# Differential attention: one pair block of scores split into a block for each map

## What is computed

```python
def diff_attention(q, k, v, lam):
    scale = HEAD_DIM ** -0.5

    def block(j, qb):
        logits = jnp.einsum("bqhmd,bkhmd->bhmqk", qb, k).astype(jnp.float32) * scale
        p = jax.nn.softmax(logits, axis=-1)
        a = (p[:, :, 0] - lam * p[:, :, 1]).astype(v.dtype)
        return jnp.einsum("bhqk,bkhd->bqhd", a, v)
...
    q, k = axial_rope(q, ang), axial_rope(k, ang)
...
    o = finish(diff_attention(q, jnp.concatenate([kc, k], axis=1),
                              jnp.concatenate([vc, v], axis=1), lam), s)
    oc = finish(diff_attention(qc, kc, vc, lam), n_ctx) if need_ctx else None
```

## Time and profile before

| | us |
|---|---|
| median of 3 runs | 3616.75 |
| lowest, highest | 3615.14, 3618.65 |
| the profiled execution | 3619.0 |
| its span, first to last instruction | 3617.2 |
| TensorE busy in the span | 3279.7 (91%) |
| VectorE, ScalarE, GpSimd busy | 1588.1, 1343.1, 1172.8 |
| mean granted TensorE clock | 0.946 |

### The profile page before, as it was taken

How to read it: one execution, slowest core, us unless ns; L and a number is a source line. 1 busy time by engine, 2 the same in 40 slices (tenths; PEclk the granted TensorE clock), 3 DMA queues, 4 the chain that set the end, 5 groups by cost and what they waited for, 6 DMA issues and landing times. The chain is left out here.

```text
span 3617.2 us, 51819 instructions
## 1 busy us (share of the span) xinstructions
PE 3279.7 (91%) x20604; PEld 2645.7 (73%) x20604; DVE 1588.1 (44%) x2713; ACT 1343.1 (37%) x2419; POOL 1172.8 (32%) x612
## 2 busy tenths in 40 slices
PE   7976799998976999999999999988999987889998
PEld 6843588786743788788878788867788866678687
DVE  4954534315864434212247520037522338743374
ACT  3241333323241333224246432237532226734363
POOL 3522344344422444433310232223233411225202
PEclk9986899999986999998999999999999999999999
DMA  4343122223343222222200111110012210012102
GB/s 138 112 140 140 59 93 94 90 94 97 109 147 117 70 94 96 90 89 64 79 19 2 36 58 54 64 44 31 30 59 71 88 37 1 1 47 89 57 2 71
DMA packets 80662, 259.97 MB, mean 72 GB/s; under 512 B 11808, under 2 KB 13600, under 8 KB 80416
## 3 DMA queue, kind: packets, MB, share of 16 engines
q1 hardware_dynamic: 80416, 256.58, 21.4%
HBM read 239.24 MB, written 2.10 MB: 67 GB/s over the span
## 5 line engine op out<-in xcount | busy, mean ns | idle before, releaser
L148 PE MATMUL ps<-hs,WS 128*128 128x512 f32 (+1 forms) x8352 | 1712.6, 366 | 34.5 <-POOL WS L139 20.3
L148 PEld LDWEIGHTS ps<-hs,WS 128*128 128x128 f32 x8352 | 1422.3, 189 | 335.6 <-POOL WS L139 32.8
L139 POOL TENSOR_TENSOR WS<-W,WS 128x1024 fp32r<-128x1024 f32 x336 | 816.9, 2433 | 1440.7 <-ACT WS L132 1440.7
L132 ACT CAST WS<-W 128x1024 fp32r<-128x1024 f32 x336 | 351.2, 1047 | 653.4 <-PE ps L148 533.6
L1419 ACT ACTIVATE prob<-ps,low 128x768 f32<-128x768 f32 (+4 forms) x320 | 223.4, 700 | 190.0 <-DVE low L1489 187.8
L951 PE MATMUL ps<-kk,qq 64*128 64x256 f32 (+3 forms) x2064 | 222.7, 344 | 69.6 <-ACT prob L1155 34.2
L951 PEld LDWEIGHTS ps<-kk,qq 64*128 64x128 f32 x2064 | 164.7, 193 | 137.5 <-issue 70.1
L1489 DVE TENSOR_REDUCE low<-ps 128x1 f32<-128x768 f32 (+4 forms) x320 | 216.6, 702 | 58.1 <-PE ps L951 53.7
L148 PE MATMUL ps<-WS,hs 128*128 128x512 f32 (+2 forms) x1248 | 235.7, 349 | 6.7 <-POOL WS L139 3.6
L148 PE MATMUL ps<-glu,WS 128*128 128x512 f32 x1056 | 240.6, 390 | 0.0
L148 PEld LDWEIGHTS ps<-WS,hs 128*128 128x128 f32 x1248 | 202.7, 189 | 38.9 <-POOL WS L139 7.3
(11 more groups left out here) (258 smaller groups left out, 3260.4 us busy)
## 6 DMA issues: line engine op xcount, KB each, us to landing
W<-in_stream_dram SPq DMA_DIRECT2D x432, 512.0 KB, 3.5
swap<-prj SPq DMA_DIRECT2D x168, 64.0 KB, 2.2
band<-in_bias_band_dram SPq DMA_DIRECT2D x8, 512.0 KB, 3.3
prj<-prj SPq DMA_DIRECT2D x64, 64.0 KB, 2.8
xT<-in_x_dram SPq DMA_DIRECT2D x4, 512.0 KB, 8.4
W<-in_stream_dram SPq DMA_DIRECT2D x1, 2048.0 KB, 13.2
out_dram<-xT SPq DMA_DIRECT2D x8, 256.0 KB, 2.7
xT<-in_ctx_dram SPq DMA_DIRECT2D x1, 1024.0 KB, 6.1
```

Of the source, the lines that this page charges most:

```text
L132: nc.scalar.copy(WS[:, j % 2, 0, :], M.W[:, (pos + j) % RING, :]).then_inc(high, 1)
L139: nc.gpsimd.tensor_tensor(WS[:, j % 2, 1, :], M.W[:, (pos + j) % RING, :], WS[:, j % 2, 0, :], ALU.subtract).then_inc(split, 1)
L148: last = pe.matmul(out, a(i), b(j), start=start and n == 0, stop=stop and n == 2)
```

## The change

The pair block of scores is split. A new routine `map_scores` issues the six products (three for each range of keys) of one map. TensorE's step x is now: map 0's scores of x, the transposes of x - 2, map 1's scores of x, the value products of x - 3. For latent works map 0's scores wait for one exponential of the work before (`exped` 2x - 1), map 1's for both. `scored` is counted once for each map, and VectorE waits for it before each of the two maxima; ScalarE's wait before it overwrites a group's queries counts twice as far.

```diff
+    def map_scores(self, pe, out, hd, s, s_keys, q0, keys):
+
+        half = slice(64 * hd, 64 * hd + 64)
+        for kc, sc, c in keys:
+            for n, (i, j) in enumerate(((0, 0), (1, 0), (0, 1))):
+                last = pe.matmul(out[:, sc:sc + c], self.qq[half, s, i, q0:q0 + P],
+                                 self.kk[half, s_keys, j, kc:kc + c], start=n == 0, stop=n == 2)
+        return last
...
+                def map_scores(pe, x, hd):
+                    g, p, m, keys, _ = works[x]
+                    if x:
+                        pe.wait_ge(exped, max(1, W.exps_ahead(x) - (0 if W.double(x) else 1 - hd)))
+                    operands.map_scores(pe, W.scores(M, x, hd), hd, g % 2, g % 2, m * P // 2, keys
+                                        ).then_inc(scored, 1)
...
-                        if x:
-                            pe.wait_ge(exped, max(1, W.exps_ahead(x)))
-                        operands.scores(pe, lambda hd: W.scores(M, x, hd), g % 2, g % 2, m * P // 2, keys
-                                        ).then_inc(scored, 1)
+                        map_scores(pe, x, 0)
...
                         last.then_inc(turned, 1)
+                    if x < X:
+                        map_scores(pe, x, 1)
...
-                                act.wait_ge(scored, W.start[g - 1])
+                                act.wait_ge(scored, 2 * W.start[g - 1])
...
-                            if hd == 0:
-                                dve.wait_ge(scored, x + 1)
+                            dve.wait_ge(scored, u + 1)
```

## The result

The changed kernel took 3647.3 us (median of 6 runs, 3633.3 to 3648.5) against 3618.9 us for the kernel before (6 runs, 3615.1 to 3621.2): a ratio of 1.0072, 95% interval 1.0056 to 1.0088. It is slower, as forecast, but by 28 us where the forecast said 8, and outside the stated range of 3619 to 3634. The profiled execution took 3647.4 us, its span 3645.6 us.

The account below looks back on a forecast made before the run. The order of steps, a 4.27 us ring TensorE, VectorE, ScalarE, TensorE, was taken as the bound. Works 0 to 10, 10 to 30, 30 to 32 and context gave 0 + 4 + 1 + 3 = +8 us: 3624.75 us, range 3619 to 3634.

Parts of the forecast that it names:

- A map block: One map's six score products on TensorE, alone on half the rows: 1.24 us, same as a pair block; low end 1.17.
- TensorE becomes the bound: Clean latent works: TensorE's own 4.78 us exceeds VectorE's 3.7 and replaces the 4.27 us ring, +0.5 us a work.
- The third work: Third of each four latent works, VectorE held by GpSimd's key copy: TensorE idles 0.85 us, a group takes 20.0 against 19.2.
- Works 10 to 32: Later latent works: +4 us for five groups in works 10 to 30, +1 us for works 30 to 32.
- VectorE would not be late for the combination: Clean works: VectorE's combination ends before TensorE reaches the transposes that need it, with 0.45 us of slack.
- the scattered half-clock stretches go: Latent works: stretches at the lower clock disappear because TensorE is now busy 95% of the time.
- about 45.6, so 0: Works 0 to 10: steady works longer, first three shorter but partly at the lower clock, so no change from 45.6 us.
- "+3" for the context works: Works 32 to 47: map 1's scores come later where a group opens, up to 0.56 us at eight openings; +3 us taken.
- by how soon the clock rises: Works 0 to 10: the margin of -1 to +3 us around the forecast of no change.
- A second held step: Rival, 10%: GpSimd's copy of the queries' low part also delays VectorE and stalls TensorE; +14 us, 3631 us.
- Weight loads within a half: Rival, 3%: in map blocks, loads within one half do not hide under products, five of six exposed; +50 us, 3667 us.
- works as meant: Rival, 7%: a map block costs about half a pair block, 0.65 us, so VectorE sets the period; -14 us, 3603 us.

Follow-up runs that it names:

- twins: Changed kernel with an unused product on the other half beside each score product, from work 34 on: 3638.4 us; in works 0 to 2 as well: 3634.1 us.

## Why the prediction was wrong, step by step

**What held.** A map block by itself costs what a pair block cost: 1.24 us forecast, 1.24 measured. TensorE becomes the bound: 4.78 forecast, 4.82 measured (transposes 0.80 as forecast, value products 1.53 for 1.50). The third work: idle 0.85 forecast, 0.83 measured, map 0's scores behind it at M + 7.05 forecast and M + 7.15 measured (3057.69; M, the start of the second maximum before, is 3050.54 here), a group of 20.0 against 20.16. Works 10 to 32: +5 forecast, +6.0 measured. That VectorE would not be late for the combination held too.

**What failed** is one clause and the two terms that rest on it: "the scattered half-clock stretches go, since TensorE is now busy 95% of the time", and in the sum "about 45.6, so 0" for works 0 to 10 and "+3" for the context works. The scattered stretches did go in works 10 to 30, but the clock was down where the half-row blocks make up most of TensorE's work.
- Works 0 to 10: the ten works were to take 45.6 us, which leaves 45.6 - 6 x 4.82 = 16.7 us for the first four. They took 4.36 + 4.36 + 6.15 + 7.66 = 22.5 us, nearly all at the lower clock. With twins in the first three they took 3.71 + 3.39 + 4.50 + 4.74 = 16.3 us, and works 0 to 10 came to 45.3. The forecast's -1 to +3 "by how soon the clock rises" was the right doubt with too narrow a bound: the earlier trace rows already had 13.7 us at clock 0.50, and nothing in them said that blocks on half of the rows would not make it longer.
- Context works: the order's part was right (+2.6 for +3, by both profiles with twins), the clock's +8.0 was missing. I had weighed only that TensorE's 2.1 us stay under the 2.4 us of a work; at the lower clock they are 3.64, and then the stage is TensorE's own.

The profiled execution's excess (3647.4 against 3627.0 forecast for it, 20.4 us) divides into 5.9 at the start and 7.6 in the context works, 1.0 in works 10 to 32, 4.7 ahead of the stage and 1.2 behind it. The last two lie in code that the change does not touch. What moved them is not settled; the time up to the first maximum was 2970.5 to 2978.7 us over the twelve profiles of kernels that leave the code ahead as it was.

**The rivals.** A second held step did not appear: GpSimd's copy of the queries' low part (3068.95, 1.29 us) was followed by a work of normal length. Weight loads within a half do hide, as the earlier trace rows said. The Trainium skill ("TensorE: Matmul & The Clock Gate", Part 3, The mechanism) has them overlap only where the row group differs (the same section also lets a load go ahead into a background buffer). By the rule alone this is not so here: in the block at 3062.48 the 512-wide products, all within one half, start 0.23 us apart (3062.82, 3063.05, 3063.28), 2.2 columns a ns as full-array products do in the earlier trace rows, and the load that begins at 3063.05 lies under a product that runs to 3063.44. The measurement decides against it. The rival "works as meant" was rejected for the right reason as the change stands, since its condition (a block under 0.98 us) was not met. But I took the price of a block for a property of the block; it hangs on the neighbour. With the maps' blocks side by side they cost 0.91 each (1.82 / 2), under that bound, and the kernel took 3606.9 us. That this is near the 3603 given to that rival is partly luck: there a block was to cost 0.65 us.

**What stays open.** Why the clock falls for 3.4 to 13.7 us at varying places in nearly every kernel here; why one profile of the changed order (and, by its mean clock, one run of the changed kernel, 3633.3 us) kept the higher clock in the context works without twins; and how much of the 15 us between the lowest and the highest of the changed kernel's first six runs is either (3648.5 us came with a mean clock of 0.942, 3633.3 with 0.947). No number here says how much of the array has to work for the clock to rise; only the two cases were tried, half of the rows and all.

## What to carry to other kernels

TensorE's clock can't be read from its busy share: look at how many rows the products use, and price a stage of half-row products at either clock. Products that use different halves belong next to each other, alternated where possible; work of another array mode put between them costs the overlap and two changes of mode. An earlier start for one of two halves is worth having, here 0.30 us a work, if the other half follows at once.

## What the runs showed of the hardware

- Context works with half-row products alone: TensorE busy 26.00 of 26.00 us at clock 0.50, in two of three profiles. With twins on the other half: 1.00, in two of two. The stage's start at half rows: 23.9 us at the lower clock; with twins in three works 3.4, at full rows 3.4. A start given the higher clock lost it 2.3 us after the first maximum.
- Two blocks on different halves, 1.24 us each apart, take 1.82 us when they touch, without any alternation, and 1.24 alternated.
- A work with four changes between half-row and full-row products took about 0.6 us more than one with full-row products alone (4.82 against 4.23 us).
- A VectorE step on 128x1 elements took 1.61 us instead of 0.22 beside GpSimd's copy; with two reductions ahead of it moved one work on, it ran before the copy, and works 10 to 30 took 8.9 us less. A combination of 128x768 took 1.45 us instead of 1.01 beside GpSimd's clamp of 0.61.
